# A two-layer latent-token trunk on one core: squares per column block behind each residual add, and rows turned by products with a diagonal of reciprocals

## The reference, cut to what matters

```python
def rms_norm(x, g):
    xf = x.astype(jnp.float32)
    y = xf * lax.rsqrt(jnp.mean(xf * xf, axis=-1, keepdims=True) + NORM_EPS)
    return (y * g.astype(jnp.float32)).astype(x.dtype)

def modulate(xn, shift, scale):
    return xn * (1 + scale) + shift

# per layer i (0: attention and RWKV mixer, 1: convolution module)
hn_lat = modulate(rms_norm(h_lat, norm1_g[i]), m_lat[0], m_lat[1])
y_lat = mixer(hn_lat)
h_lat = h_lat + m_lat[2] * y_lat
h_lat = h_lat + m_lat[5] * squared_relu_mlp(modulate(rms_norm(h_lat, norm2_g[i]), m_lat[3], m_lat[4]), mlp_w1[i], mlp_w2[i])
```

## Time and profile before

| what | value |
|---|---|
| median of 3 runs | 3682.23 us (3679.92 to 3686.18) |
| the profiled execution | 3666.82 us |
| its span | 3665.1 us |
| TensorE products busy | 3309.7 us, 90% of the span |
| TensorE weight loads busy | 2687.5 us, 73% |
| VectorE busy | 1891.9 us, 52% |
| ScalarE busy | 1365.5 us, 37% |
| GpSimd busy | 91.8 us, 3% |
| moved by DMA | 651.24 MB, mean 178 GB/s |
| the chain that ended last | TensorE 82% of the span, DMA 7%, VectorE 5%, issue 3%, ScalarE 1% |

### The profile page before, as it was taken

One profiled execution on the slowest core, in us unless ns is written; L12 is line 12 of the kernel. 1 busy time (PEld: TensorE's weight loads), 2 busy tenths in 40 slices (PEclk: granted clock), 3 DMA queues, 4 the chain that ended last, 5 costly groups with the idle time before them and its releaser, 6 DMA issues.

```text
span 3665.1 us, 49547 instructions
## 1 busy us (share of the span) xinstructions
PE 3309.7 (90%) x19488; PEld 2687.5 (73%) x19488; DVE 1891.9 (52%) x2244; ACT 1365.5 (37%) x1581; POOL 91.8 (3%) x148
## 2 busy tenths in 40 slices
PE   5799997667998889988899999997998899999999
PEld 1588986336766666767688888887986688888787
DVE  0522321656555554645555555555897555555554
ACT  1321211334544444543333333333454333333332
POOL 1000000010000000000000000000000000000000
PEclk8799998677999999999899999998999999999999
DMA  9643431774555455556655555556530565555553
GB/s 357 213 130 122 161 119 47 258 218 137 194 183 184 172 193 195 185 186 209 195 190 178 195 184 195 184 195 184 184 115 30 177 185 194 184 192 178 194 175 135
DMA packets 320212, 651.24 MB, mean 178 GB/s; under 512 B 15499, under 2 KB 20321, under 8 KB 316641
## 3 DMA queue, kind: packets, MB, share of 16 engines
q1 hardware_dynamic: 300000, 597.04, 48.3%
q0 software_dynamic: 8896, 35.95, 4.0%
q10 hardware_dynamic: 11104, 15.01, 1.2%
HBM read 634.22 MB, written 13.60 MB: 177 GB/s over the span
## 4 chain that ended last, share of the span: by engine, by line
PE 82%; DMA 7%; DVE 5%; issue 3%; ACT 1%; ACTq 0%; POOL 0%; SPq 0%; POOLq 0%; DVEq 0%
PE ps L420 42%; PE ps L438 12%; PE ps L440 6%; PE ps L1231 6%; DMA raw<-in_ada_w_dram 4%; PE ps L361 3%; PE ps L1274 3%; PE ps L1787 2%; DMA gate<-mod_scratch 2%; PE ps L2169 1%; PE ps L1287 1%; DMA at_qk<-qkv_scratch 1%; PE ps L1332 1%; PE ps L1214 1%; DVE tmpa L476 1%
## 5 line engine op out<-in xcount | busy, mean ns | idle before, releaser
L397 DVE TENSOR_TENSOR split_lo<-raw,split_hi 128x2048 fp32r<-128x2048 f32 (+1 forms) x372 | 850.1, 2288 | 1087.3 <-ACT split_hi L387 1045.5
L387 ACT ACTIVATE split_hi<-raw 128x2048 fp32r<-128x2048 f32 (+1 forms) x372 | 710.4, 1911 | 1320.3 <-PE ps L420 973.5
L438 PE MATMUL ps<-xa,split_hi 128*128 128x512 f32 x2048 | 722.6, 397 | 23.2 <-issue 15.5
L440 PE MATMUL ps<-xa,split_lo 128*128 128x256 f32 x2048 | 576.5, 281 | 1.8 <-issue 1.8
L438 PEld LDWEIGHTS ps<-xa,split_hi 128*128 128x128 f32 x2048 | 386.0, 188 | 108.3 <-issue 18.1
L420 PE MATMUL ps<-split_hi,hT_lo 128*128 128x512 f32 x1024 | 398.4, 389 | 0.0
L420 PE MATMUL ps<-split_lo,hT_hi 128*128 128x512 f32 x1024 | 398.4, 389 | 0.0
L420 PE MATMUL ps<-split_hi,hT_hi 128*128 128x512 f32 x1024 | 398.4, 389 | 0.0
L440 PEld LDWEIGHTS ps<-xa,split_lo 128*128 128x128 f32 x2048 | 389.1, 190 | 11.6 <-issue 11.6
L361 PE MATMUL ps<-raw,s 128*32 128x512 f32 x1536 | 224.2, 674 | 50.2 <-DMA raw<-in_ada_w_dram 50.1
L420 PEld LDWEIGHTS ps<-split_hi,hT_hi 128*128 128x128 f32 x1024 | 192.2, 188 | 40.2
(11 more groups left out here) (328 smaller groups left out, 4457.8 us busy)
## 6 DMA issues: line engine op xcount, KB each, us to landing
raw<-in_mlp_w_dram SPq DMA_DIRECT2D x256, 1024.0 KB, 5.1
raw<-in_ada_w_dram SPq DMA_DIRECT2D x192, 1024.0 KB, 8.3
raw<-in_mix_in_w_dram SPq DMA_DIRECT2D x48, 1024.0 KB, 5.2
raw<-in_conv_pw_w_dram SPq DMA_DIRECT2D x48, 1024.0 KB, 5.3
gate<-mod_scratch POOLq DMA_DIRECT2D x16, 1024.0 KB, 8.0
raw<-in_mix_out_w_dram SPq DMA_DIRECT2D x16, 1024.0 KB, 5.3
qkv_scratch<-hbuf ACTq DMA_DIRECT2D x20, 256.0 KB, 3.9
rwkv_scratch<-hbuf ACTq DMA_DIRECT2D x18, 256.0 KB, 2.2
```

The lines of the kernel that those rows point to most:

```text
L387: nc.scalar.activation(split_hi[:, c, :, 0:n], raw[:, c, :, 0:n], ACT.Copy).then_inc(hi_done, 1)
L397: nc.vector.tensor_tensor(split_lo[:, c, :, 0:n], raw[:, c, :, 0:n], split_hi[:, c, :, 0:n], ALU.subtract).then_inc(lo_done, 1)
L438: pe.matmul(ps[:, base + j, :], split_hi[:, c, kk, j * P:(j + 1) * P], both, start=(k == 0), stop=False, skip_group_check=True)
L440: mm = pe.matmul(ps[:, base + j, 0:SEQ], split_lo[:, c, kk, j * P:(j + 1) * P], xa_hi[:, k, :], start=False, stop=(k == KT - 1), skip_grou ...
```

## The change

For norms 1 to 3 the change does three things. The squares are taken per block of 512 columns, right behind the residual add of that block, except that the last block's come in the norm itself. Each pair (two token tiles) goes into two columns of `small`, with `link` after each instruction, and VectorE sums the 4 blocks in the norm. `hbuf` is no longer scaled into `xn2`: VectorE writes a diagonal of the reciprocals (`rdiag`, identity times a column, 128x128 for each token tile), and TensorE multiplies the rows of `hbuf` with it as a plain float32 product, which turns and scales them at once. In the loop over the quarters of the first MLP the squares of blocks 0 to 2 are issued in all four quarters, and only the last quarter's are used. The wait for the gate, GpSimd's queue and SyncE's queue stay as they were.

```diff
+            rdiag = sb(s, "rdiag", [P, 2, P])
-            with ExitStack() as t:
-                xn2 = sb(t, "xn2", [P, 2, D])
...
+        def pe_scaled_turns(pe, n0):
+            for i in range(KT // 2):
+                n = n0 + i
+                if n >= 4:
+                    pe.wait_ge(tr_ts, n - 3)
+                for j in range(2):
+                    for t in range(2):
+                        k = 2 * i + j
+                        o = (2 * j + t) * P
+                        mm = pe.matmul(ps[:, n % 4, o:o + P], hbuf[:, t, k * P:(k + 1) * P], rdiag[:, t, :], start=True, stop=True)
+                mm.then_inc(tr_ps, 1)
+
+        def act_squares(act, steps, k, count):
+            act.wait_ge(res_add, count)
+            for t in range(2):
+                steps.link(nc.scalar.activation(sqj[:, :], hbuf[:, t, k * NB:(k + 1) * NB], ACT.Square,
+                                                accum_out=small[:, 18 + 4 * t + k:19 + 4 * t + k]))
+
+        def act_deviation(act, steps, q):
+            squares_at[q] = steps.base + steps.n
+            act.wait_ge(norm_sum, q)
+            nc.scalar.activation(small[:, 4:6], small[:, 0:2], ACT.Sqrt, scale=1.0 / D, bias=epsc[:, 0:1]).then_inc(norm_std, 1)
+
+        def dve_rdiag(dve, q, steps):
+            dve.wait_ge(act_s, squares_at[q])
+            nc.vector.tensor_reduce(small[:, 0:2], small[:, 18:26].rearrange("p (t k) -> p t k", t=2), AX_X, ALU.add).then_inc(norm_sum, 1)
+            dve.wait_ge(norm_std, q + 1)
+            steps.link(nc.vector.reciprocal(small[:, 8:10], small[:, 4:6]))
+            for t in range(2):
+                ins = nc.vector.tensor_scalar(rdiag[:, t, :], ident[:, :], small[:, 8 + t:9 + t], None, ALU.mult)
+            ins.then_inc(norm_xn, 1)
...
                 act_split(act, M_OUT + e + 1, M_OUT + e + 1 + B_OFF)
+                if e:
+                    act_squares(act, steps, e - 1, e)
...
             def norm(q, tr0):
-                act.wait_ge(res_add, (4, 20, 24)[q - 1])
-                act_stats(act, q, hbuf, xn2, 2)
+                act_squares(act, steps, 3, (4, 20, 24)[q - 1])
+                act_deviation(act, steps, q)
...
                     if not (last and k == 7):
                         act_split(act, m + 1, m + (1 + B_OFF))
+                    if squares and k > 4:
+                        act_squares(act, steps, k - 5, i * 4 + (rbase + k - 4))
...
             with act.Fori(0, Q4) as i:
-                mlp_quarter(i, M_MLP0, 0, 4, False)
+                steps.enter(i, 6)
+                mlp_quarter(i, M_MLP0, 0, 4, False, True)
+            steps.leave(Q4)
...
                 act_split(act, M_PW2 + n + 1, M_PW2 + n + 1 + B_OFF)
+                if n:
+                    act_squares(act, steps, n - 1, 20 + n)
...
-                dve_scale(dve, q, steps, hbuf, xn2, 2)
+                dve_rdiag(dve, q, steps)
...
-                pe_transposes(pe, tr0, xn2, 2)
+                pe_scaled_turns(pe, tr0)
```

More of the change, by code:

```diff
@@ L270, in build_trunk @@
         epsc = sb(top, "epsc", [P, 2])
+        sqj = s32[:, :, :].rearrange("p k n -> p (k n)")
         prow = [hbuf[:, 0, 0:P], hbuf[:, 0, P:2 * P]]
@@ L315, in build_trunk @@
         norm_std, norm_xn, tr_ps, tr_ts, tr_hi, tr_lo = (sem(n) for n in ("norm_std", "norm_xn", "tr_ps", "tr_ts", "tr_hi", "tr_lo"))
-        norm_sq = sem("norm_sq")
+        norm_sq, norm_sum = sem("norm_sq"), sem("norm_sum")
         mix_ev_a, mix_ev_d = sem("mix_ev_a"), sem("mix_ev_d")
@@ L456, in pe_transposes @@
                 tr.then_inc(tr_ps, 1)
+        def pe_scaled_turns(pe, n0):
[9 more added lines that the diff above has]
+                mm.then_inc(tr_ps, 1)
+        squares_at = {}
+        def act_squares(act, steps, k, count):
[15 more added lines that the diff above has]
+            ins.then_inc(norm_xn, 1)
         def dve_modulate(dve, n0, tiles, cols, hi, lo):
@@ L1487, in act_rest, with mlp_quarter @@
                 act_split(act, M_OUT + e + 1, M_OUT + e + 1 + B_OFF)
+                if e:
+                    act_squares(act, steps, e - 1, e)
             def norm(q, tr0):
-                act.wait_ge(res_add, (4, 20, 24)[q - 1])
-                act_stats(act, q, hbuf, xn2, 2)
+                act_squares(act, steps, 3, (4, 20, 24)[q - 1])
+                act_deviation(act, steps, q)
                 act_high(act, tr0, 2, lambda i: xa_hi[:, 2 * i:2 * i + 2, :])
-            def mlp_quarter(i, m0, abase, rbase, last):
+            def mlp_quarter(i, m0, abase, rbase, last, squares=False):
                 for k in range(8):
```

## The result

| | before | changed |
|---|---|---|
| median, us (lowest to highest; runs) | 3682.12 (3678.02 to 3686.18; 6) | 3654.91 (3652.16 to 3660.66; 6) |
| profiled execution, us | 3666.82 | 3652.44 |
| its span, us | 3665.1 | 3650.8 |

The changed kernel is faster, by 27 us between the medians. The recorded ratio of the runs, 0.9940 (0.9926 to 0.9954), is not the quotient of the medians (0.9926); by it the gain is 22 us (17 to 27). The forecast was 3678.6 us, 3.6 less than before, within 3672 to 3686. The time lies far outside that range. The two profiled executions differ by 14.4 us. One of the twelve executions of first_loop, further down, was slow (3975.89 us, at a mean granted clock of 0.868), and its figures here leave it out.

The account below looks back on a forecast made before the run. TensorE's chain was taken as the bound, with norm 2 on it and the gate's loads ending last at norms 1 and 3. Saved 4.2 less 1.6, plus 1.0, made 3.6 us: 3682.2 to 3678.6 us, range 3672 to 3686.

Parts of the forecast that it names:

- Turning by plain products: TensorE's turn at norm 2: each product is two records, 1.70 us per group instead of 0.85; 1.6 us given back.
- Sum: Whole kernel: 2.6 us at norm 2 plus 1.0 on the gate's loads, 3.6 us less, 3678.6 us.
- Squares of the last block, sum, root, diagonals: Norm 2, from last add to first turned tile: 2.81 us instead of 7.01, saving 4.2.
- Norms 1 and 3 at zero: At norms 1 and 3 the gate's loads end last, so TensorE waits longer and the norm's saving counts 0.
- GpSimd's issues: First partial sum's issue at norms 1 and 3 shortens to about 0.87 us, bringing gate loads 1.0 us earlier in total.
- The other squares: 18 pairs behind the high parts, 1.44 us each, hidden in 3.52 us of ScalarE idle time; cost 0.
- rivals of the slow side: Two slower cases: squares not hidden, 3704 us, and turned products costing four transposes, 3718 us; chance 0.03 each.
- pair stalls the queue: Linked squares in ScalarE's queue delay the high parts at all 18 places, up to 26 us, 3704 us; chance 0.03.
- product costs four transposes: In the turns a group takes 3.41 us at half clock; all three norms later, 3718 us; chance 0.03.
- The clock: Denser turn might hold TensorE's clock up at norm 2, 3677.1 us, or lose 1 to 3 us elsewhere; chance 0.15.
- The chances: For the whole kernel's time: 0.12 faster by over 0.2%, 0.06 slower, 0.82 neither.
- all three norms paying: Rival: the gate does not bind norms 1 and 3, so each norm gives 2.6 us, 3673.4 us; chance 0.04.

Follow-up runs that it names:

- first_loop: Kernel before with 32 idle transposes ahead of norm 1 and 96 ahead of norm 3, moving only the first MLP's loop to the changed layout: 3673.65 us, ratio 0.9986.
- pad_before: Kernel before with 32 idle 32x32 transposes ahead of each later norm, giving both MLP loops the changed kernel's layout: 3659.58 us, ratio 0.9957.
- pad_after: Changed kernel with 96 idle transposes ahead of norm 1 and 64 ahead of norm 3, MLP loops back at their old block fractions: 3672.70 us, ratio 0.9993.
- turns_only: Changed kernel with only the turning by diagonal products, squares taken over 2048 columns in the norm as before: 3656.98 us, ratio 0.9947.
- late_before: layout_before with VectorE's wait for the gate moved from behind norms 1 and 3 to the gate's first use: 3595.23 us, ratio 0.9771.
- late_after: Changed kernel, 32 idle transposes in the RWKV stage and 64 ahead of norm 3, gate's wait moved to its first use: 3589.00 us, ratio 0.9754.
- squares_only: Changed kernel with only the per-block squares; scaling into `xn2` and TensorE's transposes as in the kernel before: 3676.17 us, ratio 1.0001.
- rwkv_before: Kernel before with 32 idle transposes at the start of the RWKV stage, moving its loop and both MLP loops: 3608.68 us, ratio 0.9810.
- layout_before: Kernel before with idle transposes, 32 in the RWKV stage and 32, 32, 96 ahead of norms 1 to 3: 3608.79 us, ratio 0.9809.

## Why the prediction was wrong

**The step that failed** is the part "Turning by plain products". It took from the trace that a product is two records, and priced their time, but not what two records and two weight loads are besides: 192 more instructions in TensorE's code. The **Sum** had no term for the length of the code, so it could not see that both MLP loops move against the blocks in which their code is fetched. The term that was missing is 18 us: pad_before 18.0, or 14.9 for the last loop and 5.1 for the first. The 27 us are these 18, some 2 to 5 of the edits themselves (2.4 in the trace, 4.9 by pad_after), and some 4 to 7 that no run explains and that may be scatter of the medians: the kernel before alone had medians of 3682.12, 3677.59, 3678.74 and 3679.62 in four sets of runs, and layout with turned products came to 20.6 us in turns_only. By the recorded ratios it is 22 us, of which 16 are the layout and 3 the edits, and the rest is within their intervals.

The rows were there to be read: gaps that end with "issue" at the turns of the RWKV loop and of the MLP loops, one of them 4.62 us long, and a line of the page for the queue of instructions. That the change makes TensorE's code longer follows from the two records for each product, which the prediction used. What an offset costs can't be read from a single layout, though; that took pad_before.

**Squares of the last block, sum, root, diagonals:** right, 2.85 against 2.81. The single terms: squares 0.73 each (0.72), the sum 0.17 (0.18), the diagonals 0.48 for both (0.56).

**Turning by plain products, its time:** right. The cadence of 1.70, two records for a product, and norm 2 at 2.38 (2.6).

**Norms 1 and 3 at zero:** right. The waits took up what was saved, 7.1 and 6.20 with the gate as releaser, and only with the gate's wait moved (late_before, late_after) did the change pay there.

**GpSimd's issues:** half right. They shortened as expected, but the loads did not land earlier, and this 1.0 us was not had. The three loads behind the first issue took 0.1 to 0.6 us more each at norm 1; by the spread of 38 to 41 us above this need not come from the change, and no run was made for it.

**The other squares:** right, hidden, with 2.10 us to spare. squares_only shows no loss. The rivals of the slow side did not come true: no pair stalls the queue, and no product costs four transposes.

**The clock:** it didn't decide at norm 2. It rose to 1.00 in the turn, fell while TensorE waited, and the weight block from 2515.45 on ran at half speed until 2519.4, about 3.9 us where the earlier trace rows had 3.0, so that it cost 0.4 us more (us, PE, PEld, DVE, ACT, POOL busy, clock, DMA; changed kernel):

```profile
2517.50:2518.50 1.00, 1.00 (x6) 1.00 (x6) 0.00 (x0) 0.00 (x0) 0.00 (x0) 0.50 1.02 213
2518.50:2519.50 1.00, 1.00 (x7) 1.00 (x6) 0.00 (x0) 0.00 (x0) 0.00 (x0) 0.56 0.35 74
2519.50:2520.50 1.00, 1.00 (x11) 1.00 (x10) 0.00 (x0) 0.00 (x0) 0.00 (x0) 1.00 0.00 0
```

What the prediction did not have is the clock at the loops' turns. It was low for part of every RWKV pass with gaps that was read (0.95 in the mean of the pass shown above), and for none without.

**The chances:** 0.12 for faster came from all three norms paying and from scatter. No case held anything outside the three norms, the squares' places and the gate, and a gain of 27 us had no place in any of them.

## What to carry to other kernels

Any edit that adds or removes instructions ahead of a loop moves that loop in its engine's code. Before a small time difference is explained by the edit, count the packets of the instruction queue in both profiles, and look for gaps that end with "issue" at the loops' turns and for a lower granted clock behind them. Then time the kernel before with idle instructions in place of the added ones. If the gain comes with them, it belongs to the layout, and can be had directly.

A stage's saving counts only when no other chain of waits ends behind it. Move the other wait to where its data is read, then measure the edit again.

## What the runs showed of the hardware

- TensorE's code is fetched in packets of 16384 bytes, and where a loop lies against these blocks is a cost of its own. The MLP's loop of 7.31 blocks costs 14.9 us more for its three turns (last MLP), and 5.1 us more (first MLP), when it touches nine blocks instead of eight. At a turn the second block is there 4.2 to 4.9 us after the restart in the kernel before, and code that is shorter than that ahead of the boundary leaves a gap. For this loop nine blocks and a short first piece (under 0.31 of a block) always come together, so whether the count of blocks costs anything by itself is not shown.
- The loop of 6.60 blocks was fetched whole at every pass while it touched eight (9 packets in a pass, gaps of 4.62 and 2.59 us, a mean granted clock of 0.95), and not at all when it touched seven (clock 1.00). That is worth 50.9 us (3659.58 in pad_before, 3608.68 in rwkv_before, the kernel before beside them 3677.59 and 3678.74), 45 packets fewer (177 to 132).
- A block's end lies at a fraction of 0.90 of the positions counted from the start of the compiled code, by two loops' gaps. Why there is not known from these runs.
- 32x32 transposes, placed where TensorE waits anyway, cost nothing that can be seen: 20.41 us of norm 2 in layout_before against 20.42.
